# Moving the streamed activations by 32 to 256 bytes in SBUF

## The reference

```python
h = rmsnorm(x, norm_g)
proj = jnp.einsum('bld,dn->bln', h, w_in)            # 2048 -> 14336
...
ya = jnp.einsum('blc,cd->bld', ya * jax.nn.silu(za), w_out_a)
yb = yb * jax.nn.sigmoid(jnp.einsum('blc,ce->ble', yb, w_glu) + b_glu)
yb = jnp.einsum('blc,cd->bld', yb * jax.nn.silu(zb), w_out_b)
x = x + jnp.einsum('bld,de->ble', m, w_o)
...
proj = (u @ w_in_2)                                  # 2048 -> 6432
h = h + mixed @ w_out_2
gate, up = jnp.split(u @ w_gate_up, 2, axis=-1)      # 2048 -> 11264
h = h + (jax.nn.silu(gate) * up) @ w_down            # 5632 -> 2048
```

## Time and profile before

| | |
|---|---|
| median of 2 runs | 2235.84 us |
| lowest, highest | 2234.59, 2237.08 us |
| the profiled execution | 2236.46 us |
| its span, first to last instruction | 2234.8 us |
| TensorE busy in the span | 2183.7 us (98%) |
| VectorE, ScalarE, GpSimd busy | 1571.5, 1041.6, 268.8 us |
| mean granted TensorE clock | 0.995 |

### The profile page before, as it was taken

The page is one execution under the profiler, slowest core; times in us unless marked ns, Lnnn a source line. Parts: engine busy times, 40 slices in busy tenths (PEclk is TensorE's granted clock), DMA queues, the critical chain, the costliest instruction groups (busy, mean ns, idle before and its releaser), DMA issues.

```text
span 2234.8 us, 51661 instructions
## 1 busy us (share of the span) xinstructions
PE 2183.7 (98%) x20580; PEld 2127.4 (95%) x20580; DVE 1571.5 (70%) x2060; ACT 1041.6 (47%) x1357; POOL 268.8 (12%) x178
## 2 busy tenths in 40 slices
PE   7999999999999999999999999899999999999997
PEld 7999999999999989999999888799999999999997
DVE  7899999999545678778777777676665666654444
ACT  6544444444544444565344444654434434444442
POOL 0355444444100000100010000000000000000000
PEclk9999999999999999999999999999999999999999
DMA  7555555555666655655655011355555555555653
GB/s 262 183 172 181 181 180 182 182 182 185 203 193 194 220 175 192 197 169 177 204 184 182 22 50 49 105 181 186 188 187 186 184 185 186 184 179 189 190 180 132
DMA packets 107105, 387.83 MB, mean 174 GB/s; under 512 B 12032, under 2 KB 12160, under 8 KB 106752
## 3 DMA queue, kind: packets, MB, share of 16 engines
q1 hardware_dynamic: 104400, 375.44, 51.5%
q0 software_dynamic: 2176, 9.78, 1.2%
q10 hardware_dynamic: 432, 1.21, 0.1%
HBM read 384.29 MB, written 2.10 MB: 173 GB/s over the span
## 4 chain that ended last, share of the span: by engine, by line
PE 79%; DVE 14%; issue 4%; ACT 2%; DMA 0%; DVEq 0%; SPq 0%; ACTq 0%
PE ps_main L1690 24%; PE ps_main L1692 23%; PE ps_main L1691 23%; DVE w_lo L976 6%; PE ps_aux L1926 2%; ACT w_hi L495 1%; PE ps_main L1926 1%; DVE m L1135 1%; DVE m L1136 1%; PE ps_main L1999 1%; DVE acc L1142 1%; PE ps_aux L1947 1%; DVE g_scan L1145 0%; DMA w_raw<-wmain 0%; PE ps_main L2000 0%
## 5 line engine op out<-in xcount | busy, mean ns | idle before, releaser
L976 DVE TENSOR_TENSOR w_lo<-w_raw,w_hi 128x1024 fp32r<-128x1024 f32 x718 | 918.6, 1296 | 435.6 <-ACT w_hi L495 429.9
L495 ACT ACTIVATE w_hi<-w_raw 128x1024 fp32r<-128x1024 f32 x718 | 747.9, 1047 | 719.4 <-PE ps_main L1692 680.2
L1690 PE MATMUL ps_main<-xs,w_hi 128*128 128x256 f32 x1664 | 462.9, 278 | 7.8 <-DVE w_lo L976 6.9
L1691 PE MATMUL ps_main<-xs,w_hi 128*128 128x256 f32 x1664 | 460.0, 276 | 0.0
L1692 PE MATMUL ps_main<-xs,w_lo 128*128 128x256 f32 x1664 | 460.0, 276 | 0.0
L1690 PE MATMUL ps_main<-x3s,w_hi 128*128 128x256 f32 x1408 | 395.7, 281 | 0.0
L1692 PE MATMUL ps_main<-x3s,w_lo 128*128 128x256 f32 x1408 | 395.6, 281 | 0.0
L1691 PE MATMUL ps_main<-x3s,w_hi 128*128 128x256 f32 x1408 | 395.6, 281 | 0.0
L1690 PEld LDWEIGHTS ps_main<-xs,w_hi 128*128 128x128 f32 x1664 | 312.8, 188 | 16.3 <-DVE w_lo L976 11.8
L1691 PEld LDWEIGHTS ps_main<-xs,w_hi 128*128 128x128 f32 x1664 | 312.4, 188 | 0.0
L1692 PEld LDWEIGHTS ps_main<-xs,w_lo 128*128 128x128 f32 x1664 | 312.4, 188 | 0.0
(11 more groups left out here) (422 smaller groups left out, 3778.5 us busy)
## 6 DMA issues: line engine op xcount, KB each, us to landing
w_raw<-wmain SPq DMA_DIRECT2D x622, 512.0 KB, 3.5
w_raw<-wdown SPq DMA_DIRECT2D x80, 512.0 KB, 3.7
w_raw<-wdown SPq DMA_DIRECT2D x16, 256.0 KB, 2.7
bias<-bias POOLq DMA_DIRECT2D x8, 384.0 KB, 3.4
x_res<-xt POOLq DMA_DIRECT2D x4, 512.0 KB, 7.2
out<-x_res SPq DMA_DIRECT2D x3, 512.0 KB, 2.8
x_first<-xt SPq DMA_DIRECT2D x2, 512.0 KB, 7.1
x_first<-xt ACTq DMA_DIRECT2D x2, 512.0 KB, 9.4
```

The lines of the kernel that those rows point to most:

```text
L495: nc.scalar.activation(whi[:, s, 0:width], raw[:, s, 0:width], ACT.Copy).then_inc(hi_ready, 1)
L976: V.tensor_tensor(wlo[:, s, 0:width], raw[:, s, 0:width], whi[:, s, 0:width].bitcast(F32), ALU.subtract)\
L1690: nc.tensor.matmul(out, whi[:, s, w], high[:, k, :], start=(first and kk == 0), stop=False)
L1691: nc.tensor.matmul(out, whi[:, s, w], low[:, k, :], start=False, stop=False)
```

## The change

The helper `wk` adds a number of bytes that depends on the region: 32 for regions that start below `kb` 16, 96 from 16, 128 from 32 and 192 from 48. The helper `hilo` makes two tensors, each with the shift of its own region, and the low part of `act` (the one with `FB` = 44 blocks) gets 64 bytes more. `unit` already takes a pair of tensors. What is placed with `at` stays: the ring, `x_res`, `x_raw_l`, the parameters and constants. No instruction is added or removed.

```diff
+        def shift(kb):
+
+            return 32 if kb < 16 else 96 if kb < 32 else 128 if kb < 48 else 192
+
+        def wk(name, kb, shape, dtype=F32, more=0):
+            at_ = work + int(kb * K) + shift(kb) + more
+            assert base + at_ + 4 * int(np.prod(shape)) <= nc.sbuf_usable_end, name
+            return at(name, at_, shape, dtype)
 
 
         def hilo(name, kb, blocks):
-            t = wk(name, kb, [2, blocks, L], F32R)
-            return t, t[:, 0, :, :], t[:, 1, :, :]
+            high = wk(name + "_h", kb, [blocks, L], F32R)
+            low = wk(name + "_l", kb + blocks, [blocks, L], F32R, 64 if blocks == FB else 0)
+            return (high, low), high, low
```

More of the change, by code:

```diff
@@ L160, in hybrid_kernel @@
         work = small + 14 * K + 448
-        def wk(name, kb, shape, dtype=F32):
-            assert base + work + kb * K + 4 * int(np.prod(shape)) <= nc.sbuf_usable_end, name
-            return at(name, work + int(kb * K), shape, dtype)
+        def shift(kb):
[4 more added lines that the diff above has]
+            return at(name, at_, shape, dtype)
         def hilo(name, kb, blocks):
-            t = wk(name, kb, [2, blocks, L], F32R)
-            return t, t[:, 0, :, :], t[:, 1, :, :]
+            high = wk(name + "_h", kb, [blocks, L], F32R)
+            low = wk(name + "_l", kb + blocks, [blocks, L], F32R, 64 if blocks == FB else 0)
+            return (high, low), high, low
         xs, xh, xl = hilo("xs", 0, KB)
```

## The result

The changed kernel takes 2281.95 us in the median of two runs (2280.78 and 2283.11), against 2235.84: 46.1 us more, which is 1.0206 of before. The ratio on record is 1.0247, with a 95% interval of 1.0163 to 1.0331; it isn't the ratio of these medians, and the record doesn't say how it was formed. A second measurement of the same kernel later gave 1.0264 (1.0168 to 1.036). So it is slower, by about 2.1% against the usual time of the kernel before. That lies outside the predicted range of 2198 to 2262 us and on the other side of no change.

The account below looks back on a forecast made before the run. TensorE bounds the kernel: number of triples times the time of one, plus interruptions. Only its pace was to change: 2236.5 - 27.9 = 2208.6, said as 2208 us; forecast's own range 2200 to 2217, 8-in-10 range 2198 to 2262.

Parts of the forecast that it names:

- The value of its own, 357: In `x_raw`, low part `x_raw_l` at 0 modulo 512: 357 ns a triple in one run, read as dependence on addresses.
- the long run: `x3s` and `act` after the interruption at 1480.68 us: 2095 triples expected to turn to A, 27.9 us less; chance 0.44.
- A: The faster pace in dense stretches of TensorE's three passes: 340 ns a triple; 2912 of 5536 triples before the change.
- the share of 50 in 64: Runs of triples starting with all operands at 448 modulo 512: of 64, 50 settled at A, 14 at B.
- B: The slower pace in dense stretches of TensorE's three passes: 353 ns a triple; 2624 of 5536 triples before the change.
- The remaining triples: 529 triples at B outside the long run, worth 7.0 us, expected redistributed, not removed: 0, between -7 and +7 us.
- The prices: TensorE: a triple changing from B to A gives 13.3 ns; bounds for the whole kernel were priced from such differences.
- everything at B: Bound for TensorE: all 2912 triples at A go to B, 39 us more.
- at the third value: Bound for TensorE: all triples at 357 ns, 59 us more.
- Rival 1: TensorE doesn't feel addresses; same starts give same paces: 2236 us within 3; chance 0.30, shared with changes that cancel.
- Rival 2: Unlike high and low addresses hold B; 2500 triples go from A to B: 2269, up to 2295 us; slower: 0.22.
- Rival 4: TensorE pace below 340 ns a triple, by the skill's formula 69 us less than at A; chance 0.05 under 2191 us.

Follow-up runs that it names:

- the moved-together kernel: Kernel before with `base` raised by 64 bytes, so ring and activations move alike: 2233.5 us, ratio 0.9995.
- the short executions: Executions of the unchanged kernel before, 10 of 42, that took 2205.5 to 2213.8 us; the other 32 took 2229.9 to 2241.9.
- the first pair of kernels: Against the split without shift: high and low parts alike, at 0 and 64, then 480 and 32 modulo 512 from weight tiles: 2281.78 and 2262.78 us.
- the kernel with 64 and 192: Against the split without shift: parts alike, 64 modulo 512 from weight tiles below `kb` 32, 192 from there: 2248.05 us, 1.0062.

## Why the prediction was wrong

- *What bounds the kernel, and that the pace of a triple is the only term*: right. Instruction counts, clock, VectorE and DMA rows didn't change, the split cost nothing, and the stages add up to the span.
- *That the pace depends on addresses*, read from `x_raw_l`: right, and the moved-together kernel shows that it is the distance to the ring. The value of its own, 357, was in part luck. Seven profiled kernels have `x_raw` at these distances: its first run settled at 358 in two of them and at 353 in five. The sign that holds in all seven is that none of the 14 runs was at 340.
- *The step that failed* is "I take the long run to settle at A". It carried the share of 50 in 64 over from starts at offset 448 to starts at 480/32 and 64/192, as if new addresses would draw from the same lot. Offset 448 is one of the four tried at which 340 was seen. At the offsets of the change it was not seen in any run of triples of the two profiled executions. Nor were the 64 starts 64 draws: many are a few places in loops, and the eight runs of `xs` at B are one place in eight turns. And the share told little of this start even at 448: if the short executions are those in which it goes to A, that is 10 of 42. The 64 starts told of one offset only, and the one sample of another (`x_raw`, 0 of 2 at 340) was the evidence that applied. It was read for the dependence and given too little weight for the direction.
- *The remaining triples, "0, between -7 and +7"*: wrong for the same cause. The 2912 triples at 340 went to 353 or more.
- *The prices* were right in size: 13.3 ns a triple, and the bounds "everything at B", +39 us, and "at the third value", +59 us, enclose the 44 us of the profiles. The third value is 360 where much of `xs`, `ms` and `x3s` is, and not 357; `x3s`, counted as a gain of 18.5 us of the 27.9, lost 9.5.
- *Rival 1* (addresses not felt) fell with the first pair of kernels. The Trainium skill's rule on the page "SBUF — State Buffer", section "Who interferes with whom", that TensorE never waits on anyone, is one about engines that disturb each other, and nothing here speaks against it: in the `x3s` stream of both kernels the pace was the same to 0.1 ns whether or not VectorE and ScalarE wrote to the ring. But a triple takes 340 to 360 ns with the distance between what TensorE streams and what it loads, which the page's two independent ports don't account for, and the measurement decides. That the two reads meet each other is the likely reading; no run shows it.
- *Rival 2* gave 2269 to 2295 us and had the right side and size, 2282, at a chance of 0.22. Its mechanism, unlike parts, doesn't explain the loss: equal parts at 0 are the worst case.
- *The range* ended at 2262 because I expected `ybs`, `yos` and `rwkv`, whose parts stay alike, and others to be at 340. They were at 355 and 356, and part of `yos` at 360.
- *Rival 4*, a pace below 340, fell: no dense stretch of any kernel was below it. The formula that it takes from the Trainium skill's page "TensorE: Matmul & The Clock Gate", section "Back-to-back issue gap", is given there for isolated matmuls, not for a stream of weight loads and matmuls, so the estimate of 69 us didn't apply to this kernel.
- *The chances* contain a slip: under 2191 us was given 0.05 and under 2198 us, which includes it, 0.04.
- *Open*: which part inside TensorE or its reads gives these values; why a start at a good offset goes one way or the other; why one offset can have two paces that aren't 340; why `act` at the same offsets was at 353 in one kernel and 351 in another. Only the outcomes are shown.

## What to carry to other kernels

Read the distance of matmul starts in dense stretches, not the busy share: the page of the profile showed 98% busy in all of these kernels, while a triple ranged from 340 to 360 ns. In a stream like this one, with a weight load for every matmul, keep the streamed block at 64 bytes modulo 128 from the weight tile, for both parts and both rings. Look at the pace again after every move in SBUF: here shifts of 32 to 256 bytes cost 2.1% of the kernel, and 32 bytes took `xs` from 341 to 355 ns a triple. And a share counted at one setting says little about another, least of all when most of the count is one place in a loop.

## What the runs showed of the hardware that was not expected

- A dense stream of weight load and 256-column matmul, fp32r, showed separate paces at the 2.4 GHz level (granted clock 1.00): 340.0, 350, 352, 353.3, 355, 356 and 360 ns for three in most stretches. Which of them are possible goes with the distance of the two operands: 340.0 was seen only at 64 bytes modulo 128, and 360 at 0 or where the two parts stand differently. The distance modulo 128 alone doesn't fix the value: 32 gave 350 and 416 gave 352 or 356. Between the two ends lie 5.9%.
- At a good distance there are two stable paces, 340.0 and 353.3 ns. In the kernel before, one is taken at a start and kept to the next, over 6288 matmuls, across the ends of loops and a change of tensor. That isn't so everywhere: in the kernel with 64 and 192, both good distances, the pace went from 340 to 353 at the change from `xs` to `yas` without an interruption. The same program took 2206 or 2235 us, and the one long run is the likely difference.
- A pause of 0.8 us in TensorE's stream can pay for itself: it turned `act` from 353 to 340 ns, 9.4 us, in the profiled execution of all four kernels that had it.
- In the `x3s` stream the pace didn't depend on whether VectorE was writing to the ring: 353.3 and 353.3 ns in the kernel before, 360.0 and 360.0 in the changed one.
